# Last two rows of down tiles loaded in pieces of 117 and 11, then 81, 27, 18 and 2 partitions, in place of one load on 128

## The reference, cut to what matters

```python
def run_block(args):                       # one expert e, tokens tok routed to it
    tok, e = args
    xb = h_pad[tok]
    gu = xb @ w_gate_up[e] + b_gate_up[e]          # (tokens, 1024) @ (1024, 2048)
    gate = jnp.minimum(gu[:, :EXPERT_DIM], SWIGLU_LIMIT)
    up = jnp.clip(gu[:, EXPERT_DIM:], -SWIGLU_LIMIT, SWIGLU_LIMIT)
    act = gate * jax.nn.sigmoid(SWIGLU_ALPHA * gate) * (up + 1.0)
    return act @ w_down[e] + b_down[e]             # (tokens, 1024) @ (1024, 1024)
...
y = jax.ops.segment_sum(out, slot_token, num_segments=n_tok + 1)[:n_tok]
x = x + y
```

## Time and profile before

| what | value |
|---|---|
| median of 3 runs | 1087.96 us (1086.49 to 1088.13) |
| the profiled execution's own time | 1087.61 us |
| its span, first to last instruction | 1085.5 us |
| mean granted TensorE clock | 0.986 |
| TensorE busy | 1048.6 us, 97% |
| bytes read from HBM | 429.03 MB, 396 GB/s over the span |

### The profile page before, as it was taken

The page is one execution under the profiler, slowest core; times in us unless marked ns, Lnnn a source line. Parts: engine busy times, 40 slices in busy tenths (PEclk is TensorE's granted clock), DMA queues, the critical chain, the costliest instruction groups (busy, mean ns, idle before and its releaser), DMA issues.

```text
span 1085.5 us, 12191 instructions
## 1 busy us (share of the span) xinstructions
PE 1048.6 (97%) x4830; PEld 424.3 (39%) x4830; DVE 382.1 (35%) x709; ACT 121.8 (11%) x215; POOL 15.3 (1%) x31
## 2 busy tenths in 40 slices
PE   8999999999999999999998999899989999898998
PEld 6445445344343434343432434242424333332432
DVE  3797685123232332232322222222222312232222
ACT  3115213100000001000000000000000000000001
POOL 4000000000000000000000000000000000000000
PEclk9999999999999999999998999899999999999999
DMA  9905796999999999999999999999999999999996
GB/s 328 371 38 194 280 420 259 398 430 414 427 430 429 427 429 435 429 428 432 430 429 431 430 426 430 432 430 435 432 430 429 431 432 430 431 431 424 428 428 263
DMA packets 37065, 430.44 MB, mean 397 GB/s; under 512 B 4225, under 2 KB 6401, under 8 KB 16433
## 3 DMA queue, kind: packets, MB, share of 16 engines
q1 hardware_dynamic: 35328, 427.59, 93.6%
q0 software_dynamic: 1136, 1.91, 0.5%
q10 hardware_dynamic: 576, 0.60, 0.2%
HBM read 429.03 MB, written 1.05 MB: 396 GB/s over the span
## 4 chain that ended last, share of the span: by engine, by line
PE 71%; DMA 27%; DVE 1%; SPq 1%; issue 1%; ACT 0%; ACTq 0%; DVEq 0%
PE bank L1634 29%; DMA ring<-w_gate_up_dram 24%; PE bank L1663 14%; PE bank L1559 5%; PE bank L1372 5%; PE bank L1221 4%; PE bank L1586 4%; DMA ring<-w_down_dram 3%; PE bank L1652 2%; PE bank L1513 2%; PE bank L1247 1%; PE bank L1427 1%; PE bank L1181 1%; PE bank L1612 1%; SPq L317 0%
## 5 line engine op out<-in xcount | busy, mean ns | idle before, releaser
L1634 PE MATMUL bank<-ring,scr 128*64 128x512 f32 x2032 | 475.6, 611 | 27.5 <-DMA ring<-w_gate_up_dram 27.3
L1634 PEld LDWEIGHTS bank<-ring,scr 128*64 128x64 f32 x2032 | 141.1, 140 | 325.5 <-issue 284.5
L1663 PE MATMUL bank<-ring,scr 128*64 128x512 f32 x992 | 225.1, 595 | 0.1
L1121 DVE TENSOR_TENSOR x<-bank,x 128x512 f32<-128x512 f32 x120 | 77.3, 686 | 254.6 <-PE bank L1586 254.6
L1663 PEld LDWEIGHTS bank<-ring,scr 128*64 128x64 f32 x992 | 68.8, 137 | 127.6 <-issue 122.9
L1096 DVE COPY scr<-bank 128x512 f32<-128x512 f32 x32 | 22.1, 692 | 257.9 <-PE bank L1634 257.9
L1102 DVE TENSOR_TENSOR scr<-bank,bgu 128x512 f32<-128x512 f32 x64 | 41.2, 686 | 98.6 <-PE bank L1652 98.6
L1586 PE MATMUL bank<-scr 64*128 64x512 f32 x240 | 67.7, 641 | 0.1
L583 ACT ACTIVATE scr<-bank 128x512 f32<-128x512 f32 x32 | 19.1, 598 | 383.4 <-PE bank L1634 383.4
L1559 PEld LDWEIGHTS bank<-scr,xn 128*128 128x128 f32 x480 | 54.8, 192 | 13.0 <-issue 13.0
L1559 PE MATMUL bank<-scr,xn 128*128 128x128 f32 x480 | 57.8, 278 | 0.0
(11 more groups left out here) (226 smaller groups left out, 527.9 us busy)
## 6 DMA issues: line engine op xcount, KB each, us to landing
ring<-w_gate_up_dram SPq DMA_DIRECT2D x40, 4096.0 KB, 31.5
ring<-w_down_dram SPq DMA_DIRECT2D x62, 2048.0 KB, 17.5
ring<-w_gate_up_dram SPq DMA_DIRECT2D x40, 2048.0 KB, 17.6
ring<-w_gate_up_dram SPq DMA_DIRECT2D x13, 1024.0 KB, 8.8
ring<-w_in_dram SPq DMA_DIRECT2D x12, 1024.0 KB
ring<-w_out_dram SPq DMA_DIRECT2D x4, 1024.0 KB
ring<-w_down_dram SPq DMA_DIRECT2D x4, 1024.0 KB, 29.9
ring<-w_branch_pool_dram SPq DMA_DIRECT2D x2, 1024.0 KB
```

Of the source, the lines that this page charges most:

```text
L1121: V.tensor_tensor(x[:, b, 512 * h:512 * h + 512], XY[h][:, :], x[:, b, 512 * h:512 * h + 512], ALU.add).then_inc(read[f"Y{j}"], 1)
L1634: ins = MM(GB[h][T * g:T * g + T, :], xgT[:, k, T * e:T * e + T], w[:, c0:c0 + 512], start=k == 0, stop=k == KC - 1)
L1663: ins = MM(DB[T * h:T * h + T, :], actT[e][:, c, :], v3(dn_slot[j][:, :], 4)[:, k, 512 * h:512 * h + 512], start=c == 0, stop=c == KC - 1)
```

## The change

Of the last expert's eight chunks, 0 and 1, 2 and 3, 4 and 5 are loaded as before, in loads of 1 MB on 128 partitions. Chunks 6 and 7, which were one load of 1 MB with 8 KB on each partition, become six loads: chunk 6 (0.5 MB, 4 KB on each partition) in pieces of 117 and 11 partitions, then chunk 7 (the same size) in pieces of 81, 27, 18 and 2 partitions. The pieces of one chunk share a semaphore, and TensorE waits until all of them have landed: for chunk 6 before its matmuls, and now also for chunk 7 before its own.

```diff
-        last_in = [sem(f"last_in{r}") for r in range(4)]
+        last_in = [sem(f"last_in{r}") for r in range(5)]
...
+        LAST_ROWS = ((0, 2, (P,)), (2, 4, (P,)), (4, 6, (P,)), (6, 7, (117, 11)), (7, 8, (81, 27, 18, 2)))
...
             last = sp.snap(n + 0)
-            for r in range(4):
-                if r % 2 == 0:
-                    sp.wait_ge(gu_used[r // 2], last)
-                c0 = HW * (r % 2)
-                sp.dma_start(gu_slot[r // 2][:, c0:c0 + HW], dn_src(E - 1, r // 2)[:, c0:c0 + HW]).then_inc(last_in[r], 16)
+            for r, (c0, c1, pieces) in enumerate(LAST_ROWS):
+                j = c0 // 4
+                if c0 % 4 == 0:
+                    sp.wait_ge(gu_used[j], last)
+                w0, w1 = D * (c0 - 4 * j), D * (c1 - 4 * j)
+                p0 = 0
+                for n in pieces:
+                    sp.dma_start(gu_slot[j][p0:p0 + n, w0:w1], dn_src(E - 1, j)[p0:p0 + n, w0:w1]).then_inc(last_in[r], 16)
+                    p0 += n
...
             def last_down(cs):
                 for c in cs:
-                    if c % 2 == 0:
-                        pe.wait_ge(last_in[c // 2], 16)
+                    for r, (c0, c1, pieces) in enumerate(LAST_ROWS):
+                        if c == c0:
+                            pe.wait_ge(last_in[r], 16 * len(pieces))
```

## The result

| | median | range | runs |
|---|---|---|---|
| before | 1087.74 us | 1086.24 to 1088.47 | 9 |
| after | 1089.65 us | 1088.91 to 1091.15 | 9 |

The ratio is 1.0022, with a 95% interval of 1.0013 to 1.0031. That is 2.4 us more, and the two medians lie 1.9 us apart, where 0.5 us less was forecast. The median lies above the range that I gave. The profiled execution after took 1088.91 us, the fastest of the nine, with a span of 1086.8, which is 1.3 us more than the profiled one before.

A forecast was written before the change was run, and what follows sets the result against it. TensorE and DMA were seen as almost in balance, with the end following `last_down`. Gap closed -0.52 us and all else 0 gave 1087.96 - 0.5 = 1087.5 us, range 1086.5 to 1089.0.

The forecast's parts named there:

- The removable wait: TensorE's idle time before chunk 6, until the last load lands: 0.52 us, all that this change could remove.
- the added wait: TensorE's separate wait before chunk 7's matmuls: taken as 0, with 0.04 us kept for the range.
- the 4 KB rows: 4 KB in place of 8 KB rows: 0.1 us later for chunk 7, within a 0.49 us margin, so costed at nothing.
- The first three loads are the same bytes in the same order: nothing.: The last expert's loads of chunks 0 to 5, unchanged by the edit: no effect on the time, 0 us.
- How the pieces fall on the engines.: Rows per DMA engine for chunks 6 and 7, called the unknown: near 20 on the busiest, in place of 16; costed 0.
- the rule cited there: Skill rule: a load uses the largest engine count up to 16 dividing its rows; pieces go to 13, 11, 9, 9, 9, 2.
- the wait moves from chunk 6 to chunk 7: Rival: the late DMA engine gets more rows, so TensorE waits at chunk 7; 1087.5 to 1089.0 us, chance 0.18.
- the worst case by the divisor rule: Late engine among the first two, with 25 rows: chunk 7 lands at 1077.72, the end 0.4 us later than before.
- odd pieces go to few engines, or queue up at one port: Rival at the last loads: slower, 0.2% at 36 rows on one engine, 1094.4 us at 64; chance 0.05.
- The 15-partition load: Existing tiny load, landed 0.17 us behind the last large one; taken as evidence that odd-sized loads spread widely over engines.
- SP's issues: Five more load issues on SP, 2.2 us, or 10.4 us more if odd sizes issue slowly; hidden at both ends.
- The sum: Whole kernel: gap closed -0.52 us, wait, 4 KB rows, SP and spread 0 each, together -0.5 us.

The follow-up runs named there:

- the split on 128 partitions: The changed kernel with chunks 6 and 7 each one load on all 128 partitions, each with its own wait: 1087.04 against 1087.39 us before the change, ratio 0.9998.
- the interleaved halves: The changed kernel with the last 1 MB load cut into even, then odd partitions, 8 KB rows, one wait: 1087.70 us, ratio 1.0003 to the kernel before.
- the run with 112 and 16: The changed kernel with chunks 6 and 7 each in pieces of 112 and 16 partitions: 1088.81 against 1087.26 us before the change, ratio 1.0017.
- halves of 64: The changed kernel with the last 1 MB load cut into partitions 0 to 63 and 64 to 127, 8 KB rows, one wait: 1091.38 us, ratio 1.0036.
- The quarters of 32: The changed kernel with the last 1 MB load in four pieces of 32 neighbouring partitions, 8 KB rows, one wait: 1091.58 us, ratio 1.0034 to the kernel before.
- Execution 6 of the change: The change itself, nothing altered, in one of six more profiled executions: 1089.41 us.

## Why the prediction was wrong

- **The removable wait.** Right for the one execution that it was read from, and not shown beyond it. With the split on 128 partitions TensorE has no gap from chunk 2 to chunk 7, but the interleaved halves, with one wait for the last megabyte as before, have none either: in both, the last megabyte was in over 1.5 us before TensorE wanted it. So the 0.52 us is no fixed sum that an own wait for chunk 7 gives back. The split on 128 does confirm that the added wait and the 4 KB rows cost nothing that shows.
- **"The first three loads are the same bytes in the same order: nothing."** This is the step that failed. The engines that were ahead started on the pieces at about 1069, while others were still at work on the third load, whose 8 KB packets then took 536 ns in place of 313. It landed 4.4 us behind the second load instead of 2.46, at 1075.4 instead of 1073.87, and TensorE stood before chunk 4 for 1.13 us. I had reckoned the pieces' cost only for the pieces' own landing.
- **"How the pieces fall on the engines."** The counting was right as far as it went: by the trace's semaphore records chunk 6's loads ended on 13 + 11 engines and chunk 7's on 9 + 9 + 9 + 2, as the rule cited there says. But I priced every row at 0.154 us, a time measured only on loads that span all 128 partitions. While the pieces are in flight a row takes 0.28. At that price, an estimate, 20 to 25 rows need 5.6 to 7 us instead of 3.1 to 3.9, which uses up most of what an average engine had to spare. That was 2.8 us by the landing records of the last load before (mean 1073.5), a little under the 3.2 that I took from the DMA share.
- **The rival "the wait moves from chunk 6 to chunk 7"** (0.18) came true for a small part. Chunk 7 landed at 1078.47, where the worst case by the divisor rule was 1077.72, and set the end of `last_down`. The slowed rows are enough for that, since even 16 of them at 0.28 us take 4.5 us in place of 2.5; whether the last engine also had more rows isn't told by the trace.
- **The rival "odd pieces go to few engines, or queue up at one port"** came nearest, but I gave it 0.05 and priced it by rows on one engine, with n = 36 for a loss of 0.2%. No engine had more than 25 rows by the divisor rule; it was the price of a row that nearly doubled, on all of them. The 15-partition load was evidence that a load spreads over engines, and none that its packets move at full speed: it has 32 bytes a row.
- **SP's issues.** Hidden, as forecast, though slow: nine issues took 10.5 us and not 3.9, one of them 4.25 us. SP still waited 17.7 us for the output tile, and the run with 112 and 16 loses time without most of the slow issues.
- **The sum.** In place of -0.5 us the first profile shows +1.3: 0.52 gained before chunk 6, 1.13 + 0.28 lost before chunk 4 and behind it, and 0.4 of start and small differences. The timed runs say 1.9 by the medians and 2.4 by the ratio; the rest is in executions that no profile here has caught.

What is shown, for halves of 64: the partitions that are written set it, not the reads and not the number of loads. For pieces of the change's kind: rows of 4 KB cost nothing on 128 partitions, and the loss comes without unequal rows and without most of the slow issue (112 and 16). No run interleaved such pieces. What is only argued: for pieces of 117 or 112, which reach nearly all partitions, that several engines write through one port at a time because a piece is dealt out to the engines in other blocks than a load on 128. No run showed which engine wrote where.

## What to carry to other kernels

Don't cut a load into blocks of neighbouring partitions to shift bytes from late engines to early ones: even where the count comes out right, as with 112 and 16, the packets of the load ahead slow down too. If a load must be cut, cut it along the rows with all 128 partitions in each part, or interleave the partitions. And when a change puts new traffic beside old, price the old traffic too, and read the DMA share together with the rate, as GB/s per busy engine.

## What the runs showed of the hardware beside that

TensorE's clock fell at the end of the halves of 64. The stretches:

```profile
1079.00:1080.00 1.00, 0.19 (x2) 0.19 (x4) 0.00 (x0) 0.00 (x0) 0.00 (x0) 1.00 0.00 0
1080.00:1081.00 1.00, 1.00 (x4) 0.25 (x3) 0.00 (x0) 0.00 (x0) 0.00 (x0) 0.54 0.00 0
1081.00:1082.00 1.00, 1.00 (x4) 0.24 (x2) 0.00 (x0) 0.00 (x0) 0.00 (x0) 0.50 0.00 0
1082.00:1083.00 1.00, 1.00 (x4) 0.00 (x0) 0.00 (x0) 0.00 (x0) 0.00 (x0) 0.50 0.00 0
```

TensorE had been idle for 2.50 us when chunk 6 began at 1079.81, and right behind that the granted clock was 0.50, 1.2 GHz, where it had been 1.00, 2.4 GHz. The eight records of chunks 6 and 7 took 3.47 us in place of 1.94: 1.5 us more for having waited. The quarters of 32 show the same behind an idle time of 2.05 us (granted clock 0.51 and 0.50 in the stretches from 1078 to 1080, and 2.87 + 2.54 us for 16 records in place of 3.88). Execution 6 of the change had 2.33 us of idle time and kept its clock, so the length of the idle time alone doesn't tell.
